# First block's latent scaling straight behind the first query tile's low parts, its norm sum behind value tile 1, the column of roots copied ahead of the scan

## The reference, cut to what matters

```
h = rmsnorm(x, ln1_g[i]) @ w_in[i]                    # i = 0, 1
(fq, fk, fv, ff, dq, dk, dv, c_q, c_kv, k_r) = jnp.split(h, ...)
o_fox = fox_group(fq, fk, fv, ff, fgate_b[i])         # log_sigmoid, cumsum, softmax(q k + bias) v
o_diff = diff_group(dq, dk, dv, ...)
o_mla = mla_group(rmsnorm(c_q, q_norm_g) @ w_uq, rmsnorm(c_kv, kv_norm_g) @ w_ukv, k_r, pos)
x = x + concatenate([o_fox, o_diff, o_mla]) @ w_o[i]
```

## Time and profile before

| | |
|---|---|
| median of three runs | 2473.88 us |
| profiled execution, whole / its span | 2475.09 us / 2473.4 us |
| PE busy | 2399.3 us, 97% of the span |
| DVE, ACT, POOL busy | 1307.8, 1018.9, 957.7 us (53%, 41%, 39%) |
| granted PE clock, mean | 0.99 |
| DMA, mean | 81 GB/s |
| share of PE in the chain that ended last | 87% (DVE 7%, ACT 3%) |

### The profile page before, as it was taken

One profiled execution on the slowest core, in us unless ns is written; L12 is line 12 of the kernel. 1 busy time (PEld: TensorE's weight loads), 2 busy tenths in 40 slices (PEclk: granted clock), 3 DMA queues, 4 the chain that ended last, 5 costly groups with the idle time before them and its releaser, 6 DMA issues.

```text
span 2473.4 us, 32452 instructions
## 1 busy us (share of the span) xinstructions
PE 2399.3 (97%) x12352; PEld 2002.8 (81%) x12352; DVE 1307.8 (53%) x2362; ACT 1018.9 (41%) x1789; POOL 957.7 (39%) x519
## 2 busy tenths in 40 slices
PE   9999999999989899999999999999999999999998
PEld 7886788888878678888878888888888888887766
DVE  5566588630255656875017633831462552756563
ACT  5465444432345544444333323331322332464552
POOL 5232444765532225466662323232323224331231
PEclk9999999999999999999999999999999999999999
DMA  5111345222311124532321111111111111110000
GB/s 198 52 56 69 110 160 199 94 96 100 128 68 56 58 81 150 184 138 95 111 97 60 52 45 58 52 62 66 52 60 43 52 52 52 63 53 34 35 18 34
DMA packets 54585, 200.48 MB, mean 81 GB/s; under 512 B 6176, under 2 KB 6176, under 8 KB 53664
## 3 DMA queue, kind: packets, MB, share of 16 engines
q1 hardware_dynamic: 52272, 189.27, 21.7%
q10 hardware_dynamic: 2160, 9.15, 1.0%
HBM read 196.29 MB, written 2.10 MB: 80 GB/s over the span
## 4 chain that ended last, share of the span: by engine, by line
PE 87%; DVE 7%; ACT 3%; issue 2%; POOL 1%; DMA 0%; DVEq 0%; ACTq 0%; POOLq 0%
PE ps L582 29%; PE ps L908 25%; PE ps L602 17%; PE ps L632 7%; PE ps L1039 2%; PE ps L799 2%; PE ps L1252 1%; DVE arena L2071 1%; PE ps L815 1%; POOL wl L2779 1%; DVE ps L2049 1%; PE ps L1237 1%; PE ps L1236 1%; DVE kl L2134 0%; DVE arena L2297 0%
## 5 line engine op out<-in xcount | busy, mean ns | idle before, releaser
L2779 POOL TENSOR_TENSOR wl<-wring,wh 128x1024 fp32r<-128x1024 f32 (+1 forms) x305 | 736.2, 2414 | 1183.0 <-ACT wh L1292 1152.8
L1292 ACT ACTIVATE wh<-wring 128x1024 fp32r<-128x1024 f32 (+1 forms) x305 | 316.4, 1042 | 428.1 <-PE ps L908 223.9
L582 PE MATMUL ps<-hh,wh 128*128 128x512 f32 x768 | 300.0, 391 | 2.5 <-POOL wl L2779 2.5
L582 PE MATMUL ps<-hh,wl 128*128 128x512 f32 x768 | 298.8, 389 | 0.0
L582 PE MATMUL ps<-hl,wh 128*128 128x512 f32 x768 | 298.8, 389 | 0.0
L602 PE MATMUL ps<-hh,wh 128*128 128x512 f32 (+1 forms) x472 | 201.1, 426 | 16.0 <-ACT rstd L1334 11.1
L602 PE MATMUL ps<-hh,wl 128*128 128x512 f32 (+1 forms) x472 | 188.3, 399 | 0.0
L602 PE MATMUL ps<-hl,wh 128*128 128x512 f32 (+1 forms) x472 | 187.4, 397 | 0.0
L582 PEld LDWEIGHTS ps<-hh,wh 128*128 128x128 f32 x768 | 144.1, 188 | 34.2 <-POOL wl L2779 1.8
L582 PEld LDWEIGHTS ps<-hl,wh 128*128 128x128 f32 x768 | 144.2, 188 | 30.2 <-issue 0.2
L582 PEld LDWEIGHTS ps<-hh,wl 128*128 128x128 f32 x768 | 144.1, 188 | 30.1
(11 more groups left out here) (373 smaller groups left out, 5618.7 us busy)
## 6 DMA issues: line engine op xcount, KB each, us to landing
wring<-wts SPq DMA_DIRECT2D x290, 512.0 KB, 3.3
arena<-wts SPq DMA_DIRECT2D x48, 512.0 KB, 3.7
wring<-wts SPq DMA_DIRECT2D x16, 384.0 KB, 2.9
xL<-xt SPq DMA_DIRECT2D x4, 512.0 KB, 6.3
arena<-tab SPq DMA_DIRECT2D x1, 2048.0 KB, 16.2
arena<-cv ACTq DMA_DIRECT2D x2, 1024.0 KB, 4.8
arena<-tab ACTq DMA_DIRECT2D x1, 2048.0 KB, 8.9
out_t<-xL ACTq DMA_DIRECT2D x8, 256.0 KB, 2.0
```

Source lines behind the costliest of these rows:

```text
L582: mm = nc.tensor.matmul(o[0], a, b, start=start and k == first and j == 0, stop=stop and k == last and j == 2)
L1292: nc.scalar.activation(wh[:, sn % SPLIT_SLOTS, :kn * w], raw(u)[:, :kn * w], ACT.Copy).then_inc(act_done, tick("act", ("hi", u)))
L2779: G.tensor_tensor(wl[:, sn % SPLIT_SLOTS, :kn * w], raw(u)[:, :kn * w], wh[:, sn % SPLIT_SLOTS, :kn * w].bitcast(F32), ALU.subtract).then_inc(
```

## The change

The diff has three parts, and each applies to both layers of the first block.

- PE: `norm(("ckv", l))` now stands behind value tile 1 and no longer behind value tile 3.
- ACT: `root(("ckv", l))` now stands behind the evacuation of value tile 2 and no longer in attention step 2.
- DVE: the copy of `rsc` now stands ahead of the forget gate's sum and scan, directly behind the scaling of key tile 0, and no longer behind the low parts of that tile. Both calls of `scaled` now stand directly behind the low parts of query tile 0, ahead of the first attention step, and no longer in steps 1 and 4.

```
@@ -706,7 +706,8 @@
                 tile_part("q", 0, 5, 0, KT)
                 for t in range(NT):
                     value_tile(0, t, 4 + 2 * (t % 2))
-                norm(("ckv", l))
+                    if t == 1:
+                        norm(("ckv", l))
 
                 def turn_out(k, b, *blocks):
 
@@ -1445,6 +1446,8 @@
                 split(("k", l, 1))
                 for t in range(NT):
                     evacuate_v(0, t, 4 + 2 * (t % 2))
+                    if t == 2:
+                        root(("ckv", l))
 
                 def high_out(k, b, *blocks):
                     act.wait_ge(pe_done, at("pe", "ot", l, k, blocks[-1] // 3))
@@ -1511,8 +1514,6 @@
                             act_done, tick("act"))
                         act.wait_ge(act_done, now("act"))
                         nc.scalar.activation(d, d, ACT.Exp, scale=-0.5).then_inc(act_done, tick("act", ("drs", l, m)))
-                    if s == 2:
-                        root(("ckv", l))
                     if s in splits:
                         key = splits[s]
                         if key[0] == "v":
@@ -2140,6 +2141,9 @@
                     by_root(ps[:, b, :], rs1x, x + "s", l, n)
 
                 scale_tile("k", 0, 6)
+                dve.wait_ge(pe_done, at("pe", "rsc", l))
+                V.tensor_copy(rsc.unsqueeze(2), ps[:, 4, :].rearrange("p (t c) -> p t c", t=NT)[:, :, 0:1]).then_inc(
+                    dve_done, tick("dve", ("rsc", l)))
                 dve.wait_ge(act_done, at("act", "softplus", l))
                 V.scalar_tensor_tensor(out=fgt[0:4], in0=fgx[0:4], scalar=0.0, in1=fgs[0:4],
                                        op0=ALU.min, op1=ALU.subtract).then_inc(dve_done, tick("dve"))
@@ -2148,9 +2152,6 @@
                 V.tensor_tensor_scan(out=fgc[0:4], data0=fgt[0:4], data1=fgt[0:4], initial=0.0,
                                      op0=ALU.add, op1=ALU.min).then_inc(dve_done, tick("dve"))
                 low_tile("k", 0, 6)
-                dve.wait_ge(pe_done, at("pe", "rsc", l))
-                V.tensor_copy(rsc.unsqueeze(2), ps[:, 4, :].rearrange("p (t c) -> p t c", t=NT)[:, :, 0:1]).then_inc(
-                    dve_done, tick("dve", ("rsc", l)))
                 scale_tile("q", 0, 5)
                 V.memset(fcr[:].bitcast(F32), 0.0).then_inc(dve_done, tick("dve"))
                 dve.wait_ge(dve_done, now("dve"))
@@ -2159,6 +2160,8 @@
                 V.scalar_tensor_tensor(out=fcr[96:100], in0=fgc[0:4], scalar=-8.0, in1=fcr[0:4].bitcast(F32),
                                        op0=ALU.mult, op1=ALU.subtract).then_inc(dve_done, tick("dve", ("fcr", l)))
                 low_tile("q", 0, 5)
+                scaled(("cq", l), lambda m: col("qn", 2 * l + m), cn)
+                scaled(("ckv", l), lambda m: col("kvn", l), cn)
 
                 def low_out(k, b, *blocks):
                     name = ("ot", l, k, blocks[-1] // 3)
@@ -2181,10 +2184,6 @@
 
                 def follow1(s):
 
-                    if s == 1:
-                        scaled(("cq", l), lambda m: col("qn", 2 * l + m), cn)
-                    if s == 4:
-                        scaled(("ckv", l), lambda m: col("kvn", l), cn)
                     for x, n, c, m in pieces_of(s):
                         if x != "v" and c + m == KT:
                             scale_tile(x, 2 * (s // 16) + n, 6 if x == "k" else 7)
```

More of the change, by code:

```diff
@@ L2182, in follow1 @@
                 def follow1(s):
[L2184 to L2187, removed]
                     for x, n, c, m in pieces_of(s):
```

## The result

The changed kernel takes 2458.45 us (median of 5 runs, 2456.32 to 2458.86) against 2473.96 us (5 runs, 2473.16 to 2477.48). The ratio is 0.9935 with a 95% interval of [0.9924, 0.9947]. The forecast was 2457.3 with a range of 2455.0 to 2462.5. A second set of runs gave 2456.55 against 2474.27, a ratio of 0.9928 [0.9915, 0.9942]. The profiled execution took 2458.86 us.

What follows compares the result with a forecast made beforehand. PE, busy 97% of the span, was taken to bound the kernel. The terms 3.05 + 11.06 + 4.23 - 0.5 - 1.2 = 16.6 us, off 2473.88, gave 2457.3 us, range 2455.0 to 2462.5.

Steps and rivals of the forecast that it cites:

- The two waits and the copy: PE's waits ahead of value tile 0 (3.05 us, by the copy) and query tile 1 (11.06 us) go in both blocks.
- The slow tail: PE's lower clock behind the 5.53 us waits at query tile 1 goes: 2.30 and 1.93 us, together 4.23 us.
- rival 1: The low clock comes anyway, drawn by PE's smaller waits in steps 0 and 5: 2461.5 us, chance 8%.
- The new waits: PE in each block: 0.25 us at key tile 1 in step 0, 0.6 us at a product in step 5.
- The margins in block 1: Low parts of key tile 0 move by 0.76 us on DVE; value tile 1 keeps over 1 us for bank 6.
- The scaling on DVE: New place ahead of the first scores costs 0; cq takes 1.5 us or, at worst, 4.97 (first scores 0.1 us late).
- rival 4: Slower: DVE waits for ckv's root ahead of its first scores, deciding once over 7 us late: 2475.5 us, chance 3%.

Runs made afterwards that it cites:

- the copy alone: Kernel before with only the copy of the column of roots moved ahead of the sum and the scan: 2470.42 against 2473.47 us, ratio 0.9987.
- the kernel that kept PE busy: Kernel before plus 40 unread matmuls ahead of query tile 1 in both blocks, inside the 5.53 us wait: 2476.1 against 2473.93 us, ratio 1.0008.
- everything but the copy: Changed kernel with the copy of the column back behind the low parts of key tile 0: 2462.82 against 2473.47 us, ratio 0.9949.
- `cq` alone: Kernel before with only the scaling of cq moved up behind the low parts of query tile 0: 2470.96 against 2473.47 us, ratio 0.9988.
- the run with 13 fills: Changed kernel with 13 fills of a free tile on DVE between the scaling of ckv and the first scores: 2470.74 against 2474.27 us, ratio 0.9985.

## Why the prediction was right

**The two waits and the copy.** 3.05 and 11.06 us, as forecast: both are gone in the trace, the copy alone brought 3.05 by its medians (1 to 5 by the interval), and the split of the 5.53 us into its two causes came out within 0.08 us.

**The slow tail.** 4.23 us, as forecast, and shown apart from the waits by the kernel that kept PE busy (2.3 and 2.0 us, some 0.2 us of each for the start behind a wait). But the argument beside it was too narrow. I took from one trace that 2.04 us of idle time do not bring the clock down. In three other kernels with that wait (everything but the copy, `cq` alone, PE kept busy) it did, at some 1.5 us. The case against rival 1 rested on that argument; the rival did not come true, since the heads ran at full clock in the changed kernel, but it deserved more than it was given.

**The new waits.** 0.28 us at key tile 1 for 0.25 forecast. 0.89 us at the product in step 5 for 0.6 forecast, mis-sized by 0.3. Its mechanism is as forecast (low parts, scores of step 4, exponential, copy). The copy ends 7.7 us after key tile 1 is done where I had 7.56, and PE arrives 6.9 us after it where I had 6.96: small gaps between the hand-overs, on both sides.

**The sum.** The next rows are of the chain at the start of step 6, in the kernel before and in the changed one:

```profile
83.63 0.46 PE ps L799 x2
...
722.30 0.45 PE ps L799 x2
```

```profile
75.27 0.46 PE ps L800 x2
...
708.02 0.45 PE ps L800 x2
```

From the transposes (39.21 and 679.26; 39.41 and 672.16 now) to there, the head of block 0 went from 44.42 to 35.86 us and that of block 1 from 43.04 to 35.86. That is 8.56 and 7.18 us, where the terms of the forecast give 9.02 and 7.62. The 0.45 us less in each are 0.3 us of the step 5 wait and the slower start behind waits, which the forecast put nowhere. The nine matmuls behind the wait at key tile 1 take 2.32 us and not 2.13, the product in step 5 takes 0.43 and not 0.17, and against these the 96 matmuls of the value tiles, which no wait precedes any more, take 2 x 5.76 = 11.52 us and not 11.77. The two heads gave 15.7 us of the 16.6 forecast. Outside them the trace has 0.2 us lost ahead of the first, 1.3 us lost between the heads and 2.0 us won behind the second. The lost 1.3 us lie where the granted clock is 0.97 and 0.93 and was 1.00 and 0.97 before. The second trace of the changed kernel does not have them (595.3 us for that stretch, against 595.6 before), so they are no part of the change. The 2.0 us behind the second head stand under no term of the forecast; that the whole comes so near 16.6 us is in part luck.

**The margins in block 1.** The forecast moves the low parts of key tile 0 by 0.76 us there and leaves value tile 1 over 1 us for bank 6. They end 8.46 us after the start of the transposes (680.62) and ended 6.84 after it before (686.10), so they moved by 1.6 us and left about 0.5 us. The copy's wait put the sum of the forget gates under a split on POOL, where it took 2.77 us and not 0.68 (the rows are in the last section). The forecast did not look at the next want, bank 4 for value tile 2, which without the norm sum ahead of it has a wait of 0.24 us. Nothing was lost by it in the changed kernel.

**The scaling on DVE.** At no cost, as forecast: `cq` took 2.71 us, between the 1.5 and 4.97 of the two bounds, and `ckv` was done 0.66 us before the first scores. What was wrong is the point from which rival 4 decides. It is 2.4 us of lateness and not 7. A nearer point speaks for more than the 3% it was given: in the run with 13 fills, 7.9 us of lateness left 3.5 us of the gain.

## What to carry to other kernels

When work is moved ahead in an engine's list, find the first want behind it through every engine that follows, weights that are prepared further down included; here it was ACT's split and POOL's low half and not the attention step itself. A wait that claims a buffer is removed by moving its last reader, and the next one is read off by the same walk: what was covered by the old idle time stands bare after it. Where idle stretches pull the clock, a wait's price is its length and a tail that can be there in one trace and not in the next, so read the mechanism in a trace and judge the gain by many executions.

## What was not expected of the hardware

The granted clock fell behind idle stretches of 1.99, 1.98 and 2.00 us of PE in three kernels and not behind 2.04 us in the kernel before, at the same place in the program; what decides it stays open. Behind 3.98 us it fell at once in block 0 and only 1.2 us after PE had begun again in block 1. The same program had its clock down at 0.93 in one execution and at 0.97 in another in the stretch from 250 to 300 us.

The scalings and the sum of the forget gates, DVE operations with both inputs in SBUF, end just behind a split of weights on POOL that they meet. `cq`'s two instructions, 0.75 us each when alone, took 4.97 us in their old place. By the trace the first runs from 62.91 to 65.10 and the second until 67.88, and POOL's two splits end at 64.55 and 67.33. In the new place the first ends at 52.94 and POOL's split at 52.40, and the second does not meet POOL, so both take 2.71 us. In block 1 the sum of the forget gates, 0.68 us in the kernel before, took 2.77 us in the changed one, because it now starts 0.17 us after a split and not ahead of one:

```profile
672.87 2.77 DVE L2148 SCALAR_TENSOR_TENSOR arena<-arena 4x512 f32<-4x512 f32 x1
```

```profile
672.70 2.40 POOL L2778 TENSOR_TENSOR wl<-wring,wh 128x1024 fp32r<-128x1024 f32 x1 [0.57 <-ACT wh L1293]
```

In all four cases DVE ends 0.54 or 0.55 us after the split that it met. It looks as if DVE stood until POOL was through. The low parts of query tile 0, which read PSUM, take their 1.41 us whether a split begins beside them or not, and the scan in block 0 ends 1.1 us behind the split and not 0.54, so this is no rule for all of DVE. No run tests it by itself.
